# Two-block transformer kernel: stages joined token tile by token tile, and the low halves of the weights written in two operations

## The reference, cut to what matters

```python
for l in range(2):                                   # first part: RMS norms
    x = x + rmsnorm(mixer(rmsnorm(x, g_mix_pre)) @ w_out, g_mix_post)      # three kinds of attention
    x = x + rmsnorm(cross_attention(rmsnorm(x, g_x_pre), rmsnorm(mem, g_x_mem)), g_x_post)
    gate, up = split(rmsnorm(x, g_ffn_pre) @ w_ffn_in)
    x = x + rmsnorm((silu(gate) * up) @ w_ffn_out, g_ffn_post)
# second part: layer norms, with shift, scale and gate from a conditioning vector (ada_w_2)
def update(x, y, gate, r, g, b): return layer_norm(ALPHA * x + r * gate * y, g, b)
ctx = update(ctx, ffn(modulate(ctx)), ...)           # one half-step FFN on the 256 context tokens
for i in range(2):
    x = update(x, ffn(modulate(x)), gate0, 0.5, ...)
    x = update(x, neighbourhood_attention(x, ctx) if i == 0 else short_conv(x), gate1, 1.0, ...)
    x = update(x, ffn(modulate(x)), gate2, 0.5, ...)
```

## Time and profile before

| | us |
|---|---|
| three runs | 2400.61, 2400.80, 2412.27 |
| median | 2400.80 |
| the profiled execution | 2409.35 |
| its span, first to last instruction | 2407.5 |
| PE busy in it | 2183.3 (91%) |
| POOL busy in it | 1617.9 (67%) |
| ACT busy, DVE busy | 1078.0, 938.3 |
| mean granted TensorE clock | 0.960 of full speed |

### The profile page before, as it was taken

How to read it: one execution, slowest core, us unless ns; L and a number is a source line. 1 busy time by engine, 2 the same in 40 slices (tenths; PEclk the granted TensorE clock), 3 DMA queues, 4 the chain that set the end, 5 groups by cost and what they waited for, 6 DMA issues and landing times.

```text
span 2407.5 us, 31430 instructions
## 1 busy us (share of the span) xinstructions
PE 2183.3 (91%) x10151; PEld 1762.8 (73%) x10151; DVE 938.3 (39%) x1680; ACT 1078.0 (45%) x1556; POOL 1617.9 (67%) x713
## 2 busy tenths in 40 slices
PE   6998899989987999899999999987997999777996
PEld 5876677778766877687777777776876887666875
DVE  6455546543544343533454335434103210444102
ACT  4554445345643553444444344544544443434442
POOL 5645377766353776687787779526876988656874
PEclk9999899999999999999999999998998999888998
DMA  6524367754343678576777765424655566444663
GB/s 201 149 105 167 133 231 236 265 167 152 106 157 125 233 247 285 198 280 235 258 284 248 294 197 167 126 68 125 187 187 157 175 184 209 130 147 134 185 189 106
DMA packets 135700, 447.06 MB, mean 186 GB/s; under 512 B 22507, under 2 KB 28099, under 8 KB 135609
## 3 DMA queue, kind: packets, MB, share of 16 engines
q1 hardware_dynamic: 128920, 426.62, 54.3%
q10 hardware_dynamic: 6688, 19.23, 2.4%
HBM read 444.60 MB, written 3.03 MB: 186 GB/s over the span
## 4 chain that ended last, share of the span: by engine, by line
PE 64%; issue 13%; POOL 12%; DVE 7%; ACT 2%; POOLq 0%; DMA 0%; ACTq 0%; DVEq 0%; SPq 0%
PE ps L1781 18%; PE ps L1783 18%; PE ps L1782 18%; POOL w_lo L740 12%; PE ps L2172 3%; PE ps L2010 1%; PE ps L2160 1%; DVE z L1486 1%; PE ps L2137 1%; PE ps L1929 1%; PE ps L2269 1%; PE ps L1999 1%; PE ps L2133 1%; DVE z L1483 1%; POOL ada_land L786 0%
## 5 line engine op out<-in xcount | busy, mean ns | idle before, releaser
L740 POOL TENSOR_TENSOR w_lo<-land,w_hi 128x1024 fp32r<-128x1024 f32 x654 | 1580.0, 2426 | 726.5 <-ACT w_hi L833 725.3
L833 ACT ACTIVATE w_hi<-land 128x1024 fp32r<-128x1024 f32 x654 | 690.2, 1060 | 975.2 <-PE ps L1783 837.3
L1781 PE MATMUL ps<-w_hi,h_hi 128*128 128x512 f32 (+1 forms) x1872 | 747.1, 399 | 50.5 <-issue 13.6
L1783 PE MATMUL ps<-w_hi,h_lo 128*128 128x512 f32 (+1 forms) x1872 | 735.0, 393 | 0.0
L1782 PE MATMUL ps<-w_lo,h_hi 128*128 128x512 f32 (+1 forms) x1872 | 734.4, 392 | 0.0
L1781 PEld LDWEIGHTS ps<-w_hi,h_hi 128*128 128x128 f32 x1872 | 355.7, 190 | 147.8 <-issue 32.2
L1783 PEld LDWEIGHTS ps<-w_hi,h_lo 128*128 128x128 f32 x1872 | 355.2, 190 | 75.9
L1782 PEld LDWEIGHTS ps<-w_lo,h_hi 128*128 128x128 f32 x1872 | 355.9, 190 | 70.2
L1333 DVE TENSOR_TENSOR hid_lo<-ps,hid_hi 128x512 f32 (+1 forms) x77 | 53.1, 690 | 589.0 <-ACT hid_hi L960 589.0
L1781 PE MATMUL ps<-w_hi,hid_hi 128*128 128x512 f32 x616 | 246.6, 400 | 14.3 <-DVE hid_lo L1333 9.7
L1783 PE MATMUL ps<-w_hi,hid_lo 128*128 128x512 f32 x616 | 243.2, 395 | 0.0
(11 more groups left out here) (251 smaller groups left out, 1975.8 us busy)
## 6 DMA issues: line engine op xcount, KB each, us to landing
land<-ffn_w_in_dram SPq DMA_DIRECT2D x220, 512.0 KB, 3.6
ada_land<-ada_w_dram SPq DMA_DIRECT2D x144, 512.0 KB, 4.9
land<-ffn_w_out_dram SPq DMA_DIRECT2D x110, 512.0 KB, 4.2
land<-w_ffn_in_dram SPq DMA_DIRECT2D x88, 512.0 KB, 3.7
land<-w_ffn_out_dram SPq DMA_DIRECT2D x44, 512.0 KB, 4.7
land<-na_w_qkv_dram SPq DMA_DIRECT2D x40, 512.0 KB, 4.1
land<-w_xkv_dram SPq DMA_DIRECT2D x32, 512.0 KB, 3.6
land<-w_in_dram SPq DMA_DIRECT2D x32, 488.0 KB, 3.4
```

The lines of the kernel that those rows point to most:

```text
L740: pool.tensor_tensor(w_lo[:, slot, :], land[:, slot, :], w_hi[:, slot, :].bitcast(F32), ALU.subtract).then_inc(*my.up("lo_ready"))
L833: act.activation(w_hi[:, slot, :], land[:, slot, :], ACT.Copy).then_inc(*my.up("hi_ready"))
L1781: pe.matmul(dst, lh, wh, start=first, stop=False)
L1783: done = pe.matmul(dst, ll, wh, start=False, stop=last)
```

## The change

1. A new `group_by_tile` does a group tile by tile: all four units for tile 0, then all four for tile 1. It is used for the last group before a norm (it raises `y_ready` after tile 0) and for the first group after one (`fresh`: it waits for each tile's banks and halves of `h` by themselves, and the transposes of tile 1 stand ahead of tile 0's last step). The units come free (`w_used`) only in the pass of tile 1.
2. `ffn_out` does its first four units by column half (before: its first two by tile), and its last four as tile 0 left half, tile 0 right half, tile 1. `then=` and the columns of the conditioning run before these last four.
3. `rms` and `ln` replace `post_rms` and `post_ln`. They work on tile 0 while PE still does tile 1, keep the values in their PSUM banks in place of `z`, and make 1/sqrt for each tile by itself with `root` (8 operations on PSUM, before 12 on SBUF for both tiles). The banks come free with the new `x` or the normalised `z`, later than before.
4. `make_h` works in quarters (tile x half) and in PSUM in place of `aff`; with a gain DVE multiplies first.
5. POOL writes a low half in two operations of 512 columns, with one signal after the second.
6. Group banks pair as (g % 2, g % 2 + 2); copies, gates and silu are one operation for each tile.
7. In `attend("na")`, from pair 5 on, the probabilities are turned before the next scores.
8. In the last group of `na_w_kv` the next `make_h` is done inside.

```diff
-                pool.tensor_tensor(w_lo[:, slot, :], land[:, slot, :], w_hi[:, slot, :].bitcast(F32),
-                                          ALU.subtract).then_inc(*my.up("lo_ready"))
+                for half in (slice(0, UW // 2), slice(UW // 2, UW)):
+                    done = pool.tensor_tensor(w_lo[:, slot, half], land[:, slot, half], w_hi[:, slot, half].bitcast(F32), ALU.subtract)
+                done.then_inc(*my.up("lo_ready"))
...
+            def group_by_tile(banks, width, fresh=False, after=None):
+                u = n["units"]
+                n["units"] += 4
+                for t in range(T):
+                    if fresh:
+                        name, value = free[t]
+                        pe.wait_ge(sems[name], my.at(name, value))
+                    for j in range(4):
+                        if t == 0:
+                            pe.wait_ge(sems["lo_ready"], my.at("lo_ready", u + j + 1))
+                        if fresh and j % 2 == 0:
+                            pe.wait_ge(sems["split_lo"], my.at("split_lo", n["split_lo"] - 3 + 2 * t + j // 2))
+                        for a in range(2):
+                            k = 2 * j + a
+                            if fresh and t == 0 and k == KC - 1 and later:
+                                later.pop()(1)
+                            done = product(u + j, a, k, h_hi, h_lo, {t: [(bank(banks[t], width), 0)]}, width, k == 0, k == KC - 1)
+                        if t:
+                            done.then_inc(*my.up("w_used"))
...
+                    if t == 0 and not fresh:
+                        done.then_inc(*my.up("y_ready"))
...
+            def root(dst, squares, name):
...
+                step(dve.tensor_scalar(guess.bitcast(I32), mean.bitcast(I32), -0.5, ROOT_BITS, ALU.mult, ALU.add))
+                for c in ROOT:
+                    step(dve.tensor_scalar(part, mean, guess, guess, ALU.mult, ALU.mult))
+                    last = c is ROOT[-1]
+                    ins_ = dve.tensor_scalar(dst if last else guess, part, 3.0 * c * c, guess, ALU.subtract, ALU.mult)
...
             # ffn_out, PE: the last four units
+                for half in range(2):
+                    for j in range(4):
+                        if half == 0:
+                            pe.wait_ge(sems["lo_ready"], my.at("lo_ready", u + j + 1))
+                        done = part(u + j, FC - 4 + j, {0: (half,)})
+                    done.then_inc(*my.up("y_ready"))
+                for j in range(4):
+                    part(u + j, FC - 4 + j, {1: (0, 1)}).then_inc(*my.up("w_used"))
...
             # rms, ACT
+                square_y(0, 1)
+                split(3)
                 act.wait_ge(sems["w_used"], my.at("w_used", n["w_used"]))
...
+                square_y(1, 1)
...
+                high(0)
+                high(1)
+                split(1)
+                high(2)
+                high(3)
...
             # ln, ACT
+                split(1)
+                variance(0)
+                split(2)
+                normalise(0)
+                split(1)
+                variance(1)
...
             # attend, PE
+                    ahead = which == "na" and i > NA_FILLED
+                    if ahead:
+                        turn_probs(2 * back)
+                        turn_probs(2 * back + 1)
```

More of the change, by code:

```diff
@@ L308, in build @@
             "centred",
+            "shifted",
+            "y_ready",
             "start_v",
@@ L1046, in ffn_out, with make_h @@
+            def make_h(src, gain=None, mod=None, folded=None):
+                affine, high = halves(src, gain, mod, folded)
+                for i in range(4):
+                    if gain is None and i % 2:
+                        affine(i)
+                    high(i)
             def ffn_out(w, ada=(), columns=None, then=None):
@@ L1071, in post_ln, with square_y, rms @@
-            def post_ln(src, res, units, ahead=0):
+            def square_y(t, half):
+                act.activation(rows[:, 1 + t, half * GW:(half + 1) * GW], bank(2 * t + half), ACT.Square,
+                               accum_out=stat[:, R_SQ[t] + half:R_SQ[t] + half + 1]).then_inc(*my.up("squares"))
+            def rms(units, early=False, gain=None):
+                n["made"] += T
+                n["w_used"] += units
+                if early:
+                    act.wait_ge(sems["w_used"], my.at("w_used", n["w_used"] - 4))
+                    square_y(0, 0)
+                    square_y(1, 0)
+                else:
+                    act.wait_ge(sems["y_ready"], my.next("y_ready"))
+                    square_y(0, 0)
+                act.wait_ge(sems["y_ready"], my.next("y_ready"))
+                square_y(0, 1)
+                split(3)
+                act.wait_ge(sems["w_used"], my.at("w_used", n["w_used"]))
+                if not early:
+                    square_y(1, 0)
+                square_y(1, 1)
+                if gain is None:
+                    split(1)
+                    return
+                _, high = halves("x", gain)
+                high(0)
+                high(1)
+                split(1)
+                high(2)
+                high(3)
@@ new lines, in make_h @@
+            def make_h(src, gain=None, mod=None, folded=None):
+                affine, low = halves(src, gain, mod, folded)
+                if gain is not None:
+                    for t in range(T):
+                        affine(2 * t)
+                        affine(2 * t + 1)
+                        low(2 * t)
+                        low(2 * t + 1)
+                    return
+                affine(0)
+                low(0)
+                affine(2)
+                for i in range(1, 4):
+                    low(i)
@@ L1850, in products_q @@
             def products_q(w):
[L1851 to L1854 removed]
+                group_by_tile((0, 2), GW, fresh=True)
+                group((1, 3), GW, after={2: ada_sum})
+                n["taken"] += 2
             def products_na():
@@ L2215, in attend @@
                         n["probs_copied"] += len(maps)
-                    if back is not None:
+                    if back is not None and not ahead:
                         turn_probs(2 * back)
```

537 lines of the change are left out of this document (313 added, 224 removed).

## The result

| | us | n |
|---|---|---|
| before, measured beside it | 2408.99 (2400.61 to 2414.64) | 11 |
| after | 2397.03 (2393.97 to 2404.82) | 11 |
| ratio, 95% interval | 0.995 (0.9935 to 0.9965) | |

The change makes the kernel 12 us faster, where 68 were forecast. That lies outside the range; to a change within 0.5%, about what was measured, the prediction had given 4 in 100. The profiled execution of the changed kernel has a span of 2392.5 us against 2407.5 and a mean clock of 0.97 against 0.96. In ratios, the forecast was 2333.0 / 2400.8 = 0.972.

The account below looks back on a forecast made before the run. PE, 91% busy, was taken to set the pace of the long streams, with idle time at joins. Terms 25 + 8 + 26 + 3.5 + 3 + 9 + 3.5 - 7 - 3 = 68 us gave 2333 us; 8-in-10 range 2302 to 2376.

Parts of the forecast that it names:

- `first = 4` lengthens nothing: In ffn_out, doing the first four units by column half costs no time, as silu and gate get twice the time.
- Joins: Stage changes at norms: five RMS joins from 11.5 to 5 us, 25 us saved; four layer-norm joins, 26 us saved.
- The two norms with an early `h` and layer norm: At these two norms PE still waits 2.7 us each, 3.5 us saved in all, bounds -3 and 6.
- The RMS norm with an early `h`: At this one norm, 10.35 us idle before; POOL's refill costs 3.4 us, 8 us saved, bounds 5 and 10.
- Halves on POOL: POOL's two operations per unit take 2.54 us, 0.14 more, hidden beside PE's 2.72 us per unit: cost 0.
- The rival in which POOL becomes the bound: POOL's pair outlasts PE's 2.72 us per unit in the streams; 2490 us at 1.5 us per operation; chance 0.05.
- DVE beside POOL: DVE's SBUF operations wait for a whole POOL operation; PSUM ones with pointer scalar don't, else 14 us less gained.
- The end: End of the program, 20.9 us before: tile 1 normalised at 7.9 instead of 11.6, 3.5 us saved, bounds 2 and 6.
- `ffn_out`'s last four units: In tile 0's first half PE waits 1.7 us for POOL's fourth unit, in four ffn_out: 7 us lost.
- The first stage: PE's 5.0 us wait for DVE shrinks through shorter POOL operations and rsqrt on PSUM: 3 us saved, bounds -2 and 6.
- ACT ahead of `ffn_in`: In RMS joins, square_x on ACT before the fifth unit's split gives back 0.5 us for each of the five.
- the refill gives half back: Rival: each join ends with PE waiting for POOL's fourth and fifth units, 39 us lost, 2372 us; chance 0.17.

Follow-up runs that it names:

- e1: Changed kernel with turn_hid(FG - 1) put between ffn_out's two passes over its first four units instead of behind both: 2352.23 us, ratio to before 0.9764.
- e6: Kernel before with one edit, ffn_out's first four units by tile where it had the first two: 2455.35 us, ratio 1.019.
- e5: Kernel before with one edit, each unit's low half written in two POOL operations of 512 columns: 2406.91 us, ratio 0.9996.
- e7: Kernel before with one edit, in na from the fourth turn on turn_probs stands behind the next pair's scores: 2398.5 us, ratio 0.9957.
- e8: Kernel with turn_hid between the passes, plus ffn_out's last four units for tile 0 unit by unit with both column halves: 2351.02 us, ratio to before 0.9756.

## Why the prediction was wrong, point by point

**The step that failed.** It is the sentence "`first = 4` lengthens nothing, as ACT's silu and DVE's gate get twice the time". It looked at what the longer pass gives (time for silu and gate ahead of the second half) and not at what is moved behind it. `turn_hid(FG - 1)` is moved past two more units, `split_hid` waits for it, and ACT's splits are queued behind `split_hid`. The kernel before already showed the 8.29 us of ACT waiting and how near it was: two units in the ring are 5.4 us of PE's work. With the ring known to have four slots and the pass to have four units, the cover was nil. Rows of the kernel before could have priced the step: from the transposes (0.6) through `split_hid` (0.6), ACT's queue (1.0 "issue"), one split (1.1) and one unit of POOL (2.5) it is 5.8 us from their start, or 5.2 of waiting, and 5.3 were measured (4.2 to 4.4 at the two of the first part, where ACT issues nothing in between). Times seven that is 35.5 us of waiting, and 45 to 46 in the runs of e1 and e6 with what the clock adds. The prediction put this term at nothing, and none of its rivals had it either.

**Joins.** RMS: 5.1 us measured in the join shown where 5 was said. Layer norm: 5.83 + 1.0 + 1.84 = 8.7 where 8.5 was said. These chains were right, in their mechanism too: first product behind a quarter of `h`, one more wait at tile 1.

Two other terms of the layer-norm joins were wrong and partly made up for each other. The refill was to cost 3.4 us for each join. Behind three of them PE waits 0.4 + 0.46 us for `w_lo`, behind the other one 0.72 + 1.41 (at 2063 and 2068 us). The clock was to cost 1 us. By PE's starts, the matmuls at half clock in the eight units behind these joins lose 4.4, 3.6, 2.0 and 3.8 us, where they lost 0 to 1.7 before. From the last product ahead of the join to the 97th behind it, less 0.2275 us for each, the four take 18.4 to 20.1 us before and 13.5 to 14.8 after. That is 21.5 us saved where 26 were said.

**The two norms with an early `h` and layer norm.** PE waits 2.94 and 2.96 us, the forecast left 2.7. It didn't have the 1.07 us that the transposes ahead of each now wait for DVE's `ada_o` (at 1175.31 and 1384.97), where the kernel before has no such wait.

**The RMS norm with an early `h`.** The forecast had 3.4 us for POOL's refill. Three waits of 0.81, 0.83 and 0.81 us stand there, 2.5 together, at full clock. That is 1 us better, but PE now loses more than this ahead of it, in a wait that the kernel before doesn't have there:

```profile
962.03 3.65 PE L2246 MATMUL ps<-ident,io 128*128 128x128 f32 x16 [3.89 <-DVE mcol L1897]
```

**Halves on POOL.** 2.55 for the pair against 2.54, the cadence unchanged at 2.72, and 0.9996 for the edit alone. Right. The rival in which POOL becomes the bound is refuted by e5.

**DVE beside POOL.** In a `renew` after a join:

```profile
1846.67 1.22 DVE L1664 TENSOR_TENSOR x<-z,rows 128x1024 f32<-128x1024 f32 x1
1847.92 1.23 DVE L1665 TENSOR_TENSOR x<-x,rows 128x1024 f32<-128x1024 f32 x1
1849.06 2.33 DVE L1664 TENSOR_TENSOR x<-z,rows 128x1024 f32<-128x1024 f32 x1
1851.42 2.20 DVE L1665 TENSOR_TENSOR x<-x,rows 128x1024 f32<-128x1024 f32 x1
```

Two of four run at 1.2, and the other two take 2.3 and 2.2 where the earlier trace rows has 3.43: they wait about as long as one half takes. The Trainium skill, "SBUF — State Buffer", says in its section on the two sides of SBUF that the port pair which DVE and GpSimd share is locked for the whole instruction. The trace agrees, with 1.0 to 1.1 us of waiting beside operations of 1.3 us. The `new x` operations with a pointer scalar didn't wait (1.28 us at each join, L1590), as the earlier trace rows said.

**Attention.** 9 us forecast, 10 measured alone in e7.

**The end.** 17.4 forecast, 17.3 measured.

**`ffn_out`'s last four units.** Waits of 1.63, 1.72 and 1.73 us where 1.7 was said, at three of the four places. But e8 shows no gain in taking them away: the next join is 0.8 us longer there, and the time is the same.

**The first stage.** The sign was wrong. PE waits 7.74 us for `zin` and not 5.01. DVE's tables start at 28.2 and not at 23.9, since the low halves of tile 1 now come first; `rsqrt` on PSUM and the shorter POOL operations give back some of that. The last product ahead of the first join stands at 202.20 and not at 201.33, so 1 us later where I had it 3 earlier.

**ACT ahead of `ffn_in`.** I had 0.5 us for the squares between the last quarter and the fifth unit. The join is shorter now, and the wait for `rstd`, which was hidden by it, is not: 2.2 us in two stages.

**The sum.** Forecast 68. e1, in which only the queue is mended, has 57, and the changed kernel has 12 = 57 - 45. The 11 that are still missing aren't split by any run. The traces of the kernel before and of e1, one execution of each, show where they lie, between the first products of the same stages. The forecast's 7 us for the last units of `ffn_out` are shared out by place.

| from, to (us in the trace before) | forecast | saved in e1 |
|---|---|---|
| start to 170.0 | 3 | -0.4 |
| 170.0 to 917.9, the five RMS joins | 23.2 | 27.7 |
| 917.9 to 1408.3, the three norms with an early `h` | 11.5 | -0.7 |
| 1408.3 to the end: four layer-norm joins, attention, the end | 30.3 | 28.3 |

So the sum hides errors of both signs. The RMS joins gave more than was said, although the wait for `rstd` (2.2 us, twice) stands behind two of them. The norms with an early `h` gave nothing. There e1 has the waits for `mcol` (3.14 us) and `ada_o` (1.07, twice), and the one for the load, 4.95 where it was 3.72. In `na_w_kv` PE waits 0.83, 1.79 and 2.75 us for `w_lo` in the changed kernel where 3 us were said. And one term was too small throughout: matmuls at half clock, by PE's starts, cost 22 us in the kernel before, 47 in the changed one and 36 in e1, although the mean granted clock rose from 0.960 to 0.970 and 0.972. The mean counts idle time at a low clock too, and there is less of that.

By the prediction's own test it was wrong if PE's idle time fell by less than 40 us (it fell by 22, from 224.2 to 202.2) or if waits of PE for `w_lo` passed 60 us (62.7 on the matmuls, 87.8 on the weight loads).

The rival "the refill gives half back" had the right form, waits of PE for `w_lo` in the second part of the gain, but in another place and with another cause: it put them at the joins, in POOL's speed. POOL was idle for 12 to 14 us ahead of each of the seven. Its own place, the joins, lost 0.8 to 2.1 us to the refill.

## What to carry to other kernels

An engine's list runs in order, so in a list that also feeds a ring a wait holds up the ring, however small the work behind the wait is. Where a change moves an operation of PE, look up who waits for it, what that engine has queued behind the wait, and count the finished units that are left in the ring at that moment; a pass as long as the ring leaves none. And where PE names POOL or ACT as what it waits for, read how long that engine has itself been idle, and for whom, until you find one that was busy: here the chain led from PE to POOL to ACT and back to PE.

Such waits are covered one by another. Shortening the joins laid open `rstd`; taking away the wait for `zin` laid open the squares. And a mean clock that rises doesn't say that fewer matmuls run slowly: read it from their starts.

## What the runs showed of the hardware

After a wait of 5.30 us PE's granted clock was 0.50 (1.2 GHz) for the next 14 matmuls, which start 0.43 us apart in place of 0.23. Behind the seven waits of 4.2 to 5.6 us there were 7 to 14 such matmuls, and not more behind the longer ones: 7 behind 5.31, 12 behind 4.38. The mean was 0.84 over a layer-norm join with waits of 2.23 and 2.54 us, and 1.00 in the RMS join with one of 1.80. The seven waits of 35.5 us in all cost 45 to 46 us in the runs.

Two POOL operations of 128x512 in a row take 2.55 us and one of 128x1024 takes 2.40, so writing the unit in two costs 0.15 us here. In a long run they keep this: 12 in 14.95 us, which is 2.49 for a pair.
